# Two decoder layers, a prompt and eight samples: projections in three fp32r terms on 512 columns, and the samples' work and paged attention moved

## The reference

```
h = rmsnorm(x)
layer 0: q,k,v,g,gd,mq = h @ w_in_gla ; tok = gated linear attention (4 heads, chunks of 64; samples: one recurrent step on a state)
layer 1: q,k,v,mq = h @ w_in_sb ; tok = stick-breaking attention (8 heads of 64)
         samples: over 4096 past tokens, 32 pages of 128 each, found by page_table in cache_sb_k / cache_sb_v
prompt: mk, mv = rmsnorm(mem) @ w_mem_kv (256 memory tokens) ; samples: cache_mem_k, cache_mem_v
m = softmax(rmsnorm(mq) . mk) @ mv                       4 heads of 128
x = x + concat(tok, m) @ w_out
up = rmsnorm(x) @ w_ffn_up (1024 x 5632) ; gate, val = halves of up
gate = conv of 3 taps along the sequence + bias ; x = x + (silu(gate) * val) @ w_ffn_down (2816 x 1024)
```

## Time and profile before

| | us |
|---|---|
| median of 3 runs | 1960.12 (1958.34 to 1961.43) |
| the profiled execution | 1966.98 |
| its span, first to last instruction | 1965.2 |
| granted TensorE clock, mean | 0.917 |

### The profile page before, as it was taken

The page is one execution under the profiler, slowest core; times in us unless marked ns, Lnnn a source line. Parts: engine busy times, 40 slices in busy tenths (PEclk is TensorE's granted clock), DMA queues, the critical chain, the costliest instruction groups (busy, mean ns, idle before and its releaser), DMA issues.

```text
span 1965.2 us, 27827 instructions
## 1 busy us (share of the span) xinstructions
PE 1752.1 (89%) x10347; PEld 1431.4 (73%) x10347; DVE 657.9 (33%) x873; ACT 469.1 (24%) x762; POOL 270.3 (14%) x292
## 2 busy tenths in 40 slices
PE   7899786889999999989998777978888988999977
PEld 6787664679999988878864445767777768777743
DVE  2102406031222200020027664477665674620100
ACT  3102222034444400010123321143332342000111
POOL 1000100014444400000001100023322323000000
PEclk9999859989999999999988887989988999999966
DMA  5321121213333322132211245959988988888698
GB/s 143 113 80 58 45 94 43 86 48 102 85 85 97 96 63 75 61 126 77 73 65 65 86 150 193 321 172 300 299 266 275 307 281 262 280 268 274 172 305 248
DMA packets 301175, 306.67 MB, mean 156 GB/s; under 512 B 14398, under 2 KB 224948, under 8 KB 301012
## 3 DMA queue, kind: packets, MB, share of 16 engines
q1 hardware_dynamic: 299144, 298.71, 49.0%
q0 software_dynamic: 1936, 6.76, 1.0%
HBM read 297.66 MB, written 7.94 MB: 156 GB/s over the span
## 4 chain that ended last, share of the span: by engine, by line
PE 66%; SPq 12%; DVE 8%; issue 6%; DMA 4%; ACT 3%; POOL 0%; DVEq 0%; ACTq 0%; POOLq 0%
PE PS L744 30%; PE PS L1019 15%; SPq L445 6%; PE PS L1199 4%; SPq L441 3%; PE PS L734 3%; PE PS L1173 2%; PE PS L720 2%; SPq L509 2%; PE PS L909 2%; PE PS L878 1%; PE PS L1067 1%; PE PS L994 1%; DVE prod L1895 1%; SPq L485 1%
## 5 line engine op out<-in xcount | busy, mean ns | idle before, releaser
L1019 PE MATMUL PS<-h_hi,w_parts 128*128 128x260 f32 (+1 forms) x2816 | 529.5, 289 | 15.3 <-DVE h_lo L1675 14.1
L1019 PEld LDWEIGHTS PS<-h_hi,w_parts 128*128 128x128 f32 x2816 | 448.9, 194 | 40.3 <-issue 37.6
L744 PE MATMUL PS<-big,wring 128*128 128x260 f32 (+1 forms) x1920 | 426.1, 383 | 0.3 <-ACT big L1518 0.3
L744 PEld LDWEIGHTS PS<-big,wring 128*128 128x128 f32 x1920 | 363.2, 190 | 68.1 <-issue 16.1
L1019 PE MATMUL PS<-h_lo,w_parts 128*128 128x260 f32 (+1 forms) x1408 | 373.5, 287 | 0.0
L648 POOL TENSOR_TENSOR w_parts<-wring,w_parts 128x512 fp32r<-128x512 f32 x176 | 231.6, 1317 | 629.2 <-ACT w_parts L1402 629.2
L1019 PEld LDWEIGHTS PS<-h_lo,w_parts 128*128 128x128 f32 x1408 | 273.6, 194 | 0.1
L1797 DVE TENSOR_TENSOR prod<-kring,PS 128x1024 f32<-128x1024 f32 x128 | 150.3, 1216 | 101.3 <-DMA kring<-cache_sb_k 101.1
L1402 ACT ACTIVATE w_parts<-wring 128x512 fp32r<-128x512 f32 x176 | 110.8, 632 | 298.2 <-PE PS L1019 292.4
L744 PE MATMUL PS<-hT,wring 128*128 128x260 f32 x768 | 171.0, 386 | 0.0
L744 PEld LDWEIGHTS PS<-hT,wring 128*128 128x128 f32 x768 | 147.6, 193 | 23.0
(11 more groups left out here) (258 smaller groups left out, 1501.4 us busy)
## 6 DMA issues: line engine op xcount, KB each, us to landing
kring<-cache_sb_k SPq DMA_DIRECT2D x256, 256.0 KB, 4.0
vring<-cache_sb_v SPq DMA_DIRECT2D x256, 256.0 KB, 3.7
wring<-w_ffn_up SPq DMA_DIRECT2D x100, 512.0 KB, 5.5
wring<-w_ffn_down SPq DMA_DIRECT2D x18, 1024.0 KB, 5.9
wring<-w_mem_kv SPq DMA_DIRECT2D x8, 1024.0 KB, 5.2
wring<-w_in_gla SPq DMA_DIRECT2D x8, 1024.0 KB, 5.6
wring<-w_out SPq DMA_DIRECT2D x8, 1024.0 KB, 5.3
kring<-cache_mem_k SPq DMA_DIRECT2D x32, 256.0 KB, 3.7
```

The lines of the kernel that those rows point to most:

```text
L744: last = mm(PS[:, 2 * par + c, 0:n], w[:, k, P * par:P * par + P], src[:, k0 + k, o:o + n], start=(first and k == 0), stop=(last_ and k == ...
L1019: last = mm(PS[:, 2 * m + c, 0:n], w_parts[:, q, a, k, :], h[:, 4 * q + k, o:o + n], start=(q == 0 and k == 0 and a == 0 and h is h_hi), s ...
```

## The change

1. Every projection of the prompt runs in three fp32r terms: input, values, memory keys and values, output, up and down. `fm_piece` makes one tile of 128 features; `token_panel` makes token-major values. In layer 0 and up to layer 1's values the prompt runs alone, in matmuls of 512 columns into one of four PSUM banks; layer 1's output projection and FFN run on 520 columns in two halves of 260 (`cuts`). Each half panel of weights is split: ACT writes the high part (`split`, called by `ahead`), POOL the low part, into `parts` with two slots.
2. The FFN goes in three chunks of 8, 8 and 6 feature tiles: up pieces of a chunk, then all eight down pieces of it, added to `xT`. A layer has 100 positions (pieces or half panels).
3. The samples' work of layer 0 and their layer-1 input projection, memory attention included, is a generator of 92 steps (`samples()`), run between the prompt's pieces of layer 0 from memory keys to memory attention (37 positions, `S_AT` steps at each). It reads its own weights, 70 panels of 1 MB or less, through four slots (`kring` and `vring`).
4. The paged attention is a generator of 86 steps (`paged()`), run between the pieces of layer 0's output projection and FFN and of layer 1's memory, input and value projections (100 positions, `KV_AT`). Key group g of sequence b is at step 9b+1+g, value group g at step 9b+13+g.
5. With the samples' attention ready before layer 1's output projection, the samples are 8 of the 520 columns from there, and the closing pass is gone.
6. SP follows the same list of positions: weight panel, sample panel, state loads and stores, key pages, value pages, each behind its wait. The normalised memory is stored to DRAM and loaded again for layer 1.

The core of the diff (the generators `samples` and `paged` and the counterparts on ACT, DVE and POOL are left out; they follow the same steps):

```diff
-            def dense_group(w, par, nk, src, k0, first, last_, cols):
-
-                for k in range(nk):
-                    for c, o, n in parts(cols):
-                        last = mm(PS[:, 2 * par + c, 0:n], w[:, k, P * par:P * par + P], src[:, k0 + k, o:o + n],
-                                  start=(first and k == 0), stop=(last_ and k == nk - 1))
-                return last
...
-                    own = (samples_out, samples_mean_square) if b == 9 else (None, None)
-                    block(Idx(b), downs, b < NB, b < NB + 1, True, *own)
-                pl.group += 8
-
-                samples_tail()
...
+PANELS = 50
+MEM0, IN0, V0, OUT0 = 0, 4, 10, 12
+CHUNKS = ((0, 8, 16), (8, 8, 28), (16, 6, 40))
+PIECES = 2 * PANELS
...
+S_PANEL_STEP = ([2, 3, 4, 6, 8, 9, 10, 11, 12, 13, 14, 15, 23, 24, 25, 26, 28, 29, 30, 31] + list(range(34, 56)) + list(range(57, 69))
+                + [71, 72, 73, 74, 76, 77, 78, 79, 80, 81, 82, 83, 87, 88, 89, 90])
+S_STEPS = 92
+S_PANELS = len(S_PANEL_STEP)
+S_AT = [2, 2] + [2] * 6 + [3] * 12 + [3] * 4 + [2] * 8 + [4, 3, 2, 2, 1]
+S_POS = 37
+KV_STEPS = 9 * 7 + 23
+KV_AT = [1] * 8 + [1, 1, 1, 0] * 3 + [1] * 4 + [1] * 8 + [1, 1, 1, 0] * 4 + [1] * 8 + [1, 1, 1, 0] * 3 + [1] * 8 + [1, 0] * 4 + [1] * 12 + [1] * 4
...
+        def cuts(cols):
+            return [(0, 0, SEQ)] if cols == PROMPT else [(c, HALF * c, HALF) for c in range(2)]
+        def half_src(l, j, h):
+            raw = wring[:, j % 2]
+            if j < IN0 or V0 <= j < OUT0:
+                return raw[:, 512 * h:512 * h + 512], 512
+            nk = 6 if j >= 46 else 8
+            m, q = h // 2, h % 2
+            t = raw[:, 0:nk * PCOL].rearrange("p (k n) -> p k n", k=nk)
+            return t[:, nk // 2 * q:nk // 2 * q + nk // 2, P * m:P * m + P], nk // 2 * P
...
+            def fm_piece(l, j, m, i, src, k0, cols, ready=None):
+                bank = dense(i, cols)
+                for q in range(2):
+                    h = 2 * m + q
+                    n = 4 * (PANELS * l + j) + h
+                    nk = half_src(l, j, h)[1] // P
+                    pe.wait_ge(wlo_ok, n + 1)
+                    for k in range(nk):
+                        kk = q * nk + k
+                        if ready:
+                            ready(kk)
+                        for a, hs in ((0, src), (1, src[0:1])):
+                            for c, o, w in cuts(cols):
+                                for x in hs:
+                                    last = mm(PS[:, bank + c, 0:w], parts[:, q, a, P * k:P * k + P], x[:, k0 + kk, o:o + w],
+                                              start=(q == 0 and k == 0 and a == 0 and x is src[0]),
+                                              stop=(q == 1 and k == nk - 1 and a == 1))
+                    done(n, last)
+            def token_panel(l, j, banks, src, k0, first, last_, after_half):
+                for h in range(4):
+                    n = 4 * (PANELS * l + j) + h
+                    pe.wait_ge(wlo_ok, n + 1)
+                    for t, b in enumerate(banks):
+                        for a, xs_ in ((0, src), (1, src[0:1])):
+                            for x in xs_:
+                                last = mm(PS[:, b, :], x[:, k0 + h, P * t:P * t + P], parts[:, n % 2, a, :],
+                                          start=(first and h == 0 and a == 0 and x is src[0]), stop=(last_ and h == 3 and a == 1))
+                    done(n, last)
+                    if h % 2:
+                        after_half()
...
+            def rows(r, src, n, k0=0, nk=None, first=True, last_=True):
+                nk = nk or src.shape[1]
+                if first and n % 2:
+                    B4.take(pe, ("row", n))
+                elif first and n:
+                    pe.wait_ge(s_rcopy, n // 2)
+                w = tiles8(flat2(slot(r)))
+                b = rows_bank(n)
+                for k in range(nk):
+                    last = mm(PS[32 * (k % 4):32 * (k % 4) + 32, b, 0:PCOL], src[:, k0 + k, :], w[:, k, :],
+                              start=(first and k < 4), stop=(last_ and k >= nk - 4))
+                last.then_inc(s_free[r % 4], 1)
+            def sums(n, by_token=False):
+                if n % 2:
+                    B4.read(pe, ("row", n))
+                    B6.take(pe, ("sum", n))
+                else:
+                    pe.wait_ge(s_rcopy, n // 2 + 1)
+                    if n:
+                        pe.wait_ge(s_ev, n // 2)
+                b = sums_bank(n)
+                if by_token:
+                    mm(PS[0:NB, b, 0:PCOL], selb[:, :], rowsS[:, n % 2, :], start=True, stop=True).then_inc(s_sum_done, 1)
+                    return
...
+            def at(pos):
+                if pos < S_POS:
+                    for _ in range(S_AT[pos]):
+                        next(sample_steps)
+                elif pos < S_POS + 100:
+                    for _ in range(KV_AT[pos - S_POS]):
+                        next(kv_steps)
...
+            mem_kv(0)
+            in_projection(0)
+            gla()
+            mem_prompt(0)
+            cursor.pos = S_POS
+            out_projection(0, PROMPT)
+            ffn(0, PROMPT)
+            mem_kv(1)
+            in_projection(1)
+            for _ in kv_steps:
+                assert False
+            sb_prompt()
+            mem_prompt(1)
+            out_projection(1, FULL)
+            ffn(1, FULL)
...
+            for pos in range(S_POS + 100):
+                while g < 2 * PANELS and piece_position(2 * (g - 2)) <= pos:
+                    panel(g)
+                    g += 1
+                while r < S_PANELS and sample_position(S_PANEL_STEP[r - 4]) <= pos:
+                    sample_panel(r)
+                    r += 1
...
+                while kn < 64 and (sample_position(S_PANEL_STEP[68 + kn]) if kn < 2 else
+                                   kv_position(9 * ((kn - 2) // 8) + 1 + (kn - 2) % 8)) <= pos:
+                    k_pages(kn)
+                    kn += 1
+                while vn < 64 and (sample_position(S_PANEL_STEP[66 + vn]) if vn < 2 else
+                                   kv_position(9 * ((vn - 2) // 8) + 13 + (vn - 2) % 8)) <= pos:
+                    v_pages(vn)
+                    vn += 1
...
+            def split(n):
+                g, h = n // 4, n % 4
+                l, j = g // PANELS, g % PANELS
+                if h == 0:
+                    act.wait_ge(w_in[j % 2], w_ready(l, j))
+                if n >= 2:
+                    if n % 2 == 0:
+                        act.wait_ge(half_done, n // 2)
+                    else:
+                        act.wait_ge(piece_done, (n - 1) // 2)
+                src, w = half_src(l, j, h)
+                copy(part_as(n, 0, src, w), src).then_inc(whi_ok, 1)
+            def ahead(gi):
+                if gi + 1 < 4 * PANELS:
+                    split(2 * gi + 2)
+                    split(2 * gi + 3)
...
```

More of the change, by code:

```diff
@@ L36 @@
 NMEM, MT = 256, 2
-MW = 512
 SBH, SBD = 8, 64
@@ new lines, in shaped, with dense_uses, ffn_takes @@
+        def shaped(ap, cols):
+            return ap if cols == PROMPT else ap.rearrange("p (c n) -> p c n", c=2)
+        def dense_uses(l, stage, i):
+            first = {"mem": 0, "in": 4, "v": 16, "out": 20, "ffn": 28}[stage]
+            if l == 0:
+                return (first + i) // 4 + 1
+            if stage in ("mem", "in", "v"):
+                return 24 + (first + i) // 4 + 1
+            return 29 + (first - 20 + i) // 2 + 1
+        def ffn_takes(c):
+            return sum(2 * n + 8 for _, n, _ in CHUNKS[:c])
@@ new lines, in tr_unit, with norm_step @@
+            def tr_unit(B, name, tiles):
+                B.put(pe, name)
+                for c, src in tiles:
+                    k, m = src.shape[0], src.shape[1]
+                    last = tp(PS[0:m, B.b, c:c + k], src, ident[0:k, 0:k])
+                last.then_inc(B.full, 1)
+            def norm_step(name, banks, k, nk, cols):
+                if k == 0:
+                    for B in banks:
+                        B.take(pe, ("norm",) + name)
+                pe.wait_ge(sq_ok, pl.sq + 1)
+                for c, o, w in cols:
+                    last = mm(PS[:, banks[c].b, 0:w], ones[:, :], sq[:, pl.sq % 2, o:o + w], start=(k == 0), stop=(k == nk - 1))
+                last.then_inc(sq_used, 1)
+                pl.sq += 1
@@ new lines, in mem_values @@
+            def mem_values(l, g, r):
+                if g == 0:
+                    pe.wait_ge(B6.free, B6.n)
+                if g % 2 == 0:
+                    B4.take(pe, ("sV", l, g // 2))
+                w = slot(r)
+                for mt in range(MT):
+                    for bb in range(2):
+                        j = 2 * (g % 2) + bb
+                        last = mm(PS[32 * j:32 * j + 32, 4, :], ps[:, mt, :], w[:, 2 * bb + mt, :], start=(mt == 0), stop=(mt == MT - 1))
+                last.then_inc(s_free[r % 4], 1)
@@ new lines, in _, with after_piece, mem_kv @@
```

(46 more changed lines are left out.)

3176 lines of the change are left out of this document (1716 added, 1460 removed).

## The result

| | before | after |
|---|---|---|
| median of 4 runs, us | 1960.78 (1958.34 to 1965.44) | 1913.66 (1906.22 to 1920.76) |
| the profiled execution / its span | 1966.98 / 1965.2 | 1920.76 / 1919.1 |

The ratio is 0.9757, with a 95% interval of 0.9715 to 0.9798: faster by 2.4%. The forecast was 1728, so 187 us of span are missing from the gain (1919 against 1732), and the time lies above the range.

The account below looks back on a forecast made before the run. The prediction saw computing bound the projections, loads the paged stretch, and waits in turns the attentions; 46 + 383 + 685 + 618 = 1732 us of span, a forecast time of 1728 us, own range 1665 to 1800, wider range 1620 to 1845.

Parts of the forecast that it names:

- Price of a projection: Prompt projections on 512 columns: fp32r starts 0.216 us apart, 24 of them 5.2 us a piece, against 7.05 in fp32.
- the rival at 0.239: Rival: 512-column fp32r starts take twice the 260-column distance, 0.239 us; 60 us more, 1788 us in all; chance 6%.
- wide starts over 0.23 apart: Sign that the forecast is wrong: 512-column fp32r starts more than 0.23 us apart instead of 0.216.
- Positions 0 to 7: Layer 0's memory positions: 28 us of half panels, 19 of panel steps, 13 of small steps with handshakes; 60 us.
- 8 to 23: Layer 0's input and value positions: 137 us for the twelve input positions and 46 us for the four value positions.
- Gated attention: Layer 0's gated linear attention, 76 us before: 85 us with the samples' 16 steps, range 70 to 100.
- Memory attention of layer 0: 66 us before, 20 of it the samples' own end; 12 steps, half in TensorE's gaps, cost 9; 55 us.
- The middle's SP chain: Layer 0's output projection to layer 1's values: SP's issues and slot waits set 16 us for two positions with a step.
- Output projection of layer 0: Eight output pieces with key groups alone at 5.6 us each, 45 us, and norm 9 us.
- Norm to layer 1: The step from layer 0's FFN to layer 1's memory positions: 7 us.
- Handshakes pile up: Rival: in-order waits and parts chains make the 178 steps 0.6 us dearer each, +107 us, 1835 us; chance 20%.
- TensorE stays the bound: Rival: loads and SP's queue hide under TensorE, the middle takes 630 us, the measured time is 1620 us; chance 17%.

Follow-up runs that it names:

- e3: Matmul streams by themselves behind the changed kernel's own work, alone or beside one other engine: fp32r on 512 columns 234 ns a start.
- e9: e8 with the samples' steps of the eight memory positions moved back, four instead of three at two input positions: 1790.28 us, ratio 0.9149.
- e6: e1 with seven of eight contraction tiles of each sample panel load left out after the first four loads: 1831.87 us, ratio 0.9328.
- e8: e7 and e5 together, with more fillers in stick-breaking and gated attention and the memory's gains under the last down pieces: 1791.27 us, ratio 0.9159.
- e7: e1 with filler matmuls, whose results nobody reads, where TensorE would stand in gated attention and both memory attentions: 1813.29 us, ratio 0.9234.
- e1: The changed kernel with SP issuing value pages ahead of key pages at each position: 1845.73 us, ratio 0.9399.
- e5: e1 with page numbers read ahead of the slot wait and layer 1's normalised memory loaded early: 1836.32 us, ratio 0.9358.
- e2: The changed kernel with three of four page loads of each key and value group left out after the first two groups: 1831.81 us, ratio 0.9328.
- e4: The changed kernel with prompt pieces as two matmuls of 256 columns instead of one of 512: 1913.94 us, ratio 0.9746.

## Why the prediction was wrong, step by step

The direction was right, by a chance of 94 to 5, and the size was not: 47 us of gain for 232. The steps in their order:

- *Price of a projection.* Wide fp32r starts were to be 0.216 apart and are 0.234 (e3). Taking the pass of an fp32 record for them was the error; the rival at 0.239 was the nearer one. It is 24 x 0.018 = 0.43 us a piece, and over the 110 pieces that the forecast had TensorE bound about 47 us. That is an upper estimate and no separate share: it lies within the stages below, and where SP's queue sets the pace part of it is hidden. One of the forecast's own signs of being wrong, wide starts over 0.23 apart, came true. The 520-column pieces, priced from rows of their own, were right.
- *Positions 0 to 7*, 71 for 60: the second sample step waits 11.8 us for VectorE (the first row below), behind whose split of the prompt's input it stands. "Small steps with handshakes of some 3 us" failed here. e9 shows that this wait was not a loss by itself.
- *8 to 23*, 208 for 183: pieces and value panels 7 us dearer; loads 6 (e6); what remains, some 12, lies most likely in the samples' steps and was not taken apart.
- *Gated attention* 88 for 85. The stage before ran at a clock of 0.58 and I carried that over without asking what it costs: 22 us (e8).
- *Memory attention of layer 0*, 73 for 55, and of layer 1, 50 for 32. Both sums took work out of TensorE's and VectorE's turns and left the clock as it was. The clock fell to 0.62 in layer 1 (0.77 before), and with fillers that hold it up 11 of the 18 us there come back (e7). That it fell because the samples' work no longer stood between the heads is likely, but no run shows it. In layer 0 the waits below are those of the heads (L404) and of the samples' own small results; fillers gave back only 3.
- *The middle's SP chain.* I had it: 16 us for two positions with a step, and the down positions, 8.2 forecast, took 8.1 to 8.6. What failed is the up positions, "16.2 + 11.4 for four, 6.9 each": from one feature tile's gate product to the next they took 7.9, 7.7 and 8.6 a position in the three chunks, 8.0 on the mean. As I read the timeline, one position without a step doesn't end the chain, because the late value pages hold TensorE, and with it VectorE's next key group, for which SP waits in turn. At 44 up positions that is 48 of the FFN's 61 us. I had also costed the queue as given, with a value group behind a key group, and never asked whether it had to be. With values first (e1) the same distances are 6.9 a position up and 7.1 down, so the order had lengthened both kinds. e1's 538 is the 537 that the forecast sums to for that stretch by luck: its output stage was 8 us short (54 for 62) and its FFN 8 us long (483 for 475, with down positions at 8.2 for 7.1).
- *Output projection of layer 0*, 63 for 54, and *layer 1's input and values*, 121 for 104: by the price above some 10 of these 26 us; the rest was not taken apart.
- *Norm to layer 1*, 21 for 7: the reload of the normalised memory waits for the last down piece and then stands in SP's queue behind two page groups (e5), a dependency that I had listed in point 6 of the change and costed at nothing. In layer 1's memory positions, 42 for 37, TensorE waits 9.1 us for GpSimd's parts.
- *Rivals.* "Handshakes pile up" was nearest in time (1835) and in kind, but its mechanism was spread over 178 steps; the loss sits in one queue's order, in the price of a start, in a clock and in a reload. "TensorE stays the bound" is refuted by e2: with three quarters of the page loads gone the middle is 704, not 630. "Wide fp32r runs at twice the 260-column start distance" had the start right within 2% (0.239 for 0.234); its time, 1788, missed because the rest of the sum was short.

TensorE's waits in the changed kernel from 52 to 123 and from 420 to 493 us, and in layer 1's memory positions:

```profile
PE PS L578 <- DVE hS L1876: 11.8, 1, 11.8
...
PE PS L404 <- DVE scr L2280: 16.5, 4, 5.5
PE PS L526 <- DVE prod L1916: 2.8, 2, 1.5
...
PE PS L469 <- POOL parts L1260: 9.1, 4, 6.2
```

Open: the 12 us of positions 8 to 23, some 16 of the output projection and of layer 1's input and values, and some 15 of layer 0's memory attention, where no experiment took one small wait away.

## What to carry to other kernels

When one queue issues loads for two rings, issue first for the ring whose slot comes free first: a wait at the head of an in-order queue charges everything behind it, and here the order of two loops was worth 66 us of 604 (e1). When work is taken out of a stage that waits in turns, ask what the clock of TensorE will be without it; a granted clock of 0.6 in the profile's windows is a price by itself, and filler matmuls in its gaps gave back 42 us of 260 in three stages (e8 against e1: 22, 10 and 10). Price a new form of instruction by bounds until a stream of it has been timed.

## What had not been expected of the hardware

- An fp32r matmul costs 0.457 to 0.466 ns a column at 256 to 512 columns (half of a plain fp32 record is 0.420), with GpSimd, ScalarE or VectorE at work beside it or not, and 111 ns at 128 columns, so that 512 columns bring nothing over 2 x 256 (e3, e4).
- TensorE's granted clock fell to 1.2 GHz in gated attention although it was busy for 10.00 of 10 us (355 to 365 us of e7), in a run of matmuls of 64 and 128 columns between rows of 32-column weights; with fillers of 256 columns among them, three after each of four sample sums, it stayed at 2.4 GHz (granted clock 1.00, e8 against e7).
- Giving TensorE 20 us of useless work made a 50 us stage 11 us shorter (e7).
